# Prompt logits of a hybrid decoder step: keys as half and remainder on the two halves of the partitions, queries doubled

## What is computed

```python
def gqa_attend(q, k_sel, v_sel, valid):
    b, t = q.shape[0], q.shape[1]
    qg = q.reshape(b, t, N_KV_HEADS, GROUP, HEAD_DIM).astype(jnp.float32)
    s = jnp.einsum('btngd,btknd->btngk', qg, k_sel.astype(jnp.float32)) * (HEAD_DIM ** -0.5)
    s = jnp.where(valid[:, :, None, None, :], s, -jnp.inf)
    p = jax.nn.softmax(s, axis=-1)
    o = jnp.einsum('btngk,btknd->btngd', p, v_sel.astype(jnp.float32))
    return o.reshape(b, t, ATTN_DIM).astype(q.dtype)
```

## Time and profile before

| | us |
|---|---|
| median of 3 runs (2747.8 to 2750.54) | 2749.54 |
| span of the profiled execution | 2748.0 |
| TensorE busy | 2554.6 (93%) |
| VectorE busy | 1214.8 (44%) |
| ScalarE busy | 1112.5 (40%) |
| POOL busy | 1006.6 (37%) |

### The profile page before, as it was taken

One profiled execution on the slowest core, in us unless ns is written; L12 is line 12 of the kernel. 1 busy time (PEld: TensorE's weight loads), 2 busy tenths in 40 slices (PEclk: granted clock), 3 DMA queues, 4 the chain that ended last, 5 costly groups with the idle time before them and its releaser, 6 DMA issues.

```text
span 2748.0 us, 40635 instructions
## 1 busy us (share of the span) xinstructions
PE 2554.6 (93%) x15166; PEld 2233.7 (81%) x15166; DVE 1214.8 (44%) x3074; ACT 1112.5 (40%) x1833; POOL 1006.6 (37%) x527
## 2 busy tenths in 40 slices
PE   6999999999779988999989988898999999999997
PEld 6999998879657777867876887787889888878787
DVE  4232224628654344443545666565333234322344
ACT  4222223635424343345544544664443233322332
POOL 5333433324434444322542332221224354454340
PEclk9999999999889999999999999999999999999998
DMA  5323323332234454211322221111113222232222
GB/s 173 97 92 106 113 87 111 124 127 95 90 96 145 128 154 136 87 47 54 127 75 73 78 78 47 47 55 39 47 47 115 78 94 90 100 107 94 91 71 73
DMA packets 157030, 253.34 MB, mean 92 GB/s; under 512 B 15009, under 2 KB 101282, under 8 KB 156834
## 3 DMA queue, kind: packets, MB, share of 16 engines
q1 hardware_dynamic: 154144, 247.02, 27.7%
q10 hardware_dynamic: 2690, 3.72, 0.4%
HBM read 240.34 MB, written 18.73 MB: 94 GB/s over the span
## 4 chain that ended last, share of the span: by engine, by line
PE 73%; DVE 11%; ACT 7%; issue 4%; POOL 3%; DVEq 1%; DMA 1%; ACTq 0%; SPq 0%
PE ps L1594 22%; PE ps L1596 21%; PE ps L1595 21%; PE ps L1807 2%; PE ps L1863 2%; POOL w_lo L789 1%; PE ps L1793 1%; PE ps L1729 1%; DVE ps L1159 1%; ACT w_hi L890 1%; DVE ha_lo L1161 1%; POOL kv_kr L839 1%; ACT ha_hi L940 1%; DVE s_hits L1419 1%; DVE xa L1250 1%
## 5 line engine op out<-in xcount | busy, mean ns | idle before, releaser
L789 POOL TENSOR_TENSOR w_lo<-raw,w_hi 128x1024 fp32r<-128x1024 f32 x250 | 599.5, 2400 | 833.2 <-ACT w_hi L890 832.9
L1594 PE MATMUL ps<-xna_hi,w_hi 128*128 128x288 f32 x2000 | 606.6, 303 | 14.1 <-POOL xna_lo L795 7.3
L1595 PE MATMUL ps<-xna_lo,w_hi 128*128 128x288 f32 x2000 | 596.1, 298 | 0.0
L1596 PE MATMUL ps<-xna_hi,w_lo 128*128 128x288 f32 x2000 | 595.6, 298 | 0.0
L789 POOL TENSOR_TENSOR d_lo<-raw,d_hi 128x1024 fp32r<-128x1024 f32 x90 | 214.9, 2388 | 653.0 <-ACT d_hi L890 653.0
L1594 PE MATMUL ps<-xnb_hi,w_hi 128*128 128x512 f32 x1000 | 406.5, 406 | 0.0
L1594 PEld LDWEIGHTS ps<-xna_hi,w_hi 128*128 128x128 f32 x2000 | 382.6, 191 | 27.8 <-issue 17.6
L1596 PE MATMUL ps<-xnb_hi,w_lo 128*128 128x512 f32 x1000 | 394.5, 394 | 0.0
L1595 PE MATMUL ps<-xnb_lo,w_hi 128*128 128x512 f32 x1000 | 393.9, 394 | 0.0
L1595 PEld LDWEIGHTS ps<-xna_lo,w_hi 128*128 128x128 f32 x2000 | 382.4, 191 | 0.2
L1596 PEld LDWEIGHTS ps<-xna_hi,w_lo 128*128 128x128 f32 x2000 | 381.9, 191 | 0.0
(11 more groups left out here) (331 smaller groups left out, 4101.1 us busy)
## 6 DMA issues: line engine op xcount, KB each, us to landing
raw<-in_w_gu SPq DMA_DIRECT2D x176, 512.0 KB, 3.5
raw<-in_w_d SPq DMA_DIRECT2D x88, 512.0 KB, 3.5
raw<-in_w_ring SPq DMA_DIRECT2D x74, 512.0 KB, 3.5
pages<-in_vk_pages SPq DMA_DIRECT2D x256, 128.0 KB, 2.6
idx_flat<-in_idx_pages SPq DMA_DIRECT2D x256, 32.0 KB, 2.4
idxp<-idx_flat SPq DMA_DIRECT2D x8, 1024.0 KB, 6.7
x_spill<-xa SPq DMA_DIRECT2D x1, 2304.0 KB, 8.9
xa<-x_spill SPq DMA_DIRECT2D x4, 576.0 KB, 6.0
```

What stands on the lines that cost most here:

```text
L789: g_.tensor_tensor(lo[slot][:, :, :], raw[l % 2][:, :, :], hi[slot][:, :, :].bitcast(f32), ALU.subtract).then_inc(lo_done, 1)
L1594: mm(out, shi, mhi, start=first, stop=False)
L1595: mm(out, shi, mlo, start=False, stop=False)
L1596: return mm(out, slo, mhi, start=False, stop=last)
```

## The change

A key head now has a tensor of its own, `kT[h]`, with 128 partitions: the rounded half of the keys on the head's own 64 partitions, the remainder on the other 64. It takes the same space as `kT_hi` and `kT_lo`. The queries' rounded half lies twice, on both halves of the partitions, in `qb_hi`, arranged by head and tile; `qb_lo` has the remainder on the head's own half and zeros on the other. One matmul of 128 rows then gives hi x hi plus hi x lo, a second one lo x hi. `split_mm` is no longer used for the prompt's logits.

The queries are prepared by half blocks of two tiles, in two groups of events: "qb" (ScalarE, now four copies of 64 x 256 in each half) and "ql" (VectorE, two subtractions, and four zero fills ahead of blocks 0 and 4). They stand at steps 4 and 0, and the buffer is now one of a half instead of one of a block's parity, so that "qb" waits for the logits of the same half of the block before. The keys' copies are two for each chunk, and their remainders move from POOL to VectorE (`key_remainders`), ahead of the first rotation after the keys.

```diff
@@ -188,9 +188,11 @@
             pv = [("pv", *two)] if two else []
             if s == 0:
-                groups += [[("qb", now[0])], [], []]
+                groups += [[("qb", now[0], 0), ("qb", now[0], 1)], [("ql", now[0], 0), ("ql", now[0], 1)], []]
             elif now and now[1] == 4 and now[0] + 1 in blocks:
-                groups.append([("qb", now[0] + 1)])
+                groups += [[("qb", now[0] + 1, 0)], [("ql", now[0] + 1, 0)]]
+            elif now and now[1] == 0:
+                groups += [[("qb", now[0], 1)], [("ql", now[0], 1)]]
             for i in range(max(len(qk), len(tr), 1)):
...
@@ -288,7 +290,7 @@
         chosen = lambda name: [[("exact", name)], [("room", name)]] + [[(step, b)] for b in SEARCH[name] for step in ("ties", "pick")]
         side = [[("bt", "B1", j)] for j in range(EARLY, 32)] + chosen("B1")
-        side[-4].append(("qb", 4))
+        side[-4] += [("qb", 4, 0), ("qb", 4, 1)]
         late = [[("bt", "B2", j)] for j in range(32)] + chosen("B2")
...
@@ -506,7 +508,7 @@
         iwT = [at("iwT_a", [128, WIDTH[0]], f32, H + 4608), at("iwT_b", [128, WIDTH[1]], f32, H + 7680)]
         ikT = at("ikT", [128, SEQ], f32, P)
-        kT_hi, kT_lo = at("kT_hi", [128, SEQ], f32r, P + 4096), at("kT_lo", [128, SEQ], f32r, P + 8192)
+        kT = [at(f"kT{h}", [128, SEQ], f32r, P + 4096 + 4096 * h) for h in range(2)]
         V = at("V", [128, 8, 128], f32, P + 12288)
...
@@ -544,8 +546,8 @@
               [at(f"PT_b{s}", [128, 8, 128], f32, XNB + 8192 + 4096 * s) for s in range(2)]]
         q_at = (XNA + 8192, XNB + 16384)
-        qb_hi = [[at(f"qb_hi{g}{s}", [128, 4, 128], f32r, q_at[g] + 4096 * s) for s in range(2)] for g in range(2)]
-        qb_lo = [[at(f"qb_lo{g}{s}", [128, 4, 128], f32r, q_at[g] + 4096 * s + 2048) for s in range(2)] for g in range(2)]
+        qb_hi = [[at(f"qb_hi{g}{s}", [128, 2, 2, 128], f32r, q_at[g] + 4096 * s) for s in range(2)] for g in range(2)]
+        qb_lo = [[at(f"qb_lo{g}{s}", [128, 2, 2, 128], f32r, q_at[g] + 4096 * s + 2048) for s in range(2)] for g in range(2)]
         inv = [at("inv_a", [128, 128], f32, XNA + 16384), at("inv_b", [128, 128], f32, XNB + 24576)]
...
@@ -794,27 +796,10 @@
                     g_.tensor_tensor(xn_lo[g][:, m, own(c)], xnf[g][:, m, own(c)], xn_hi[g][:, m, own(c)].bitcast(f32), ALU.subtract).then_inc(xn_pool, 1)
 
-            def product(pn, half):
-                kind, w, c, key = products[pn]
-                if kind != "in" or half < PARTS[c] - 1 or key[0] != T_K:
-                    return
-                g, (o, k) = GROUP[c], CH[c]
-                first, at_ = FIRST[c], PPOS[c]
-                pool.wait_ge(k_hi_done, c + 1)
-                z = tb[2]
-                if c == 0:
-                    g_.tensor_tensor(kn_lo[:, :], z[:, 0:NS], kn_hi[:, :].bitcast(f32), ALU.subtract)
-                g_.tensor_tensor(kT_lo[:, at_:at_ + k - first], z[:, o + first:o + k], kT_hi[:, at_:at_ + k - first].bitcast(f32), ALU.subtract).then_inc(k_ready, 1)
-
             def pad(kc):
                 if kc == 0:
                     pool.wait_ge(xnf_done, n("scale", 1, 1, KT - 1))
                     g_.memset(S0[0:64, HALF:HW], NEG).then_inc(s0_pad, 1)
-
-            def queries(b):
-                g = group(b)
-                pool.wait_ge(q_hi_done, n("qb", b))
-                g_.tensor_tensor(qb_lo[g][b % 2][:, :, :], attn[g][:, :, lcol(b):lcol(b) + 128], qb_hi[g][b % 2][:, :, :].bitcast(f32), ALU.subtract).then_inc(q_ready, 1)
 
...
@@ -849,7 +834,7 @@
                 last.then_inc(pe_ready, 1)
 
-            does = {"begin": begin, "sp": split, "scale": scale, "p": product, "sil": pad, "qb": queries, "qs": sample_queries,
+            does = {"begin": begin, "sp": split, "scale": scale, "sil": pad, "qs": sample_queries,
                     "ks": keys, "mix": mix, "pe": embed}
...
@@ -967,7 +952,9 @@
                         if c == 0:
                             A(kn_hi[:, :], tb[2][:, 0:NS], ACT.Copy)
-                        A(kT_hi[:, at_:at_ + k - first], tb[2][:, o + first:o + k], ACT.Copy).then_inc(k_hi_done, 1)
+                        for h in range(2):
+                            last = A(kT[h][64 * h:64 * h + 64, at_:at_ + k - first], tb[2][64 * h:64 * h + 64, o + first:o + k], ACT.Copy)
+                        last.then_inc(k_hi_done, 1)
                 elif t == T_V:
...
@@ -1020,15 +1007,19 @@
                     A(vn[:, :], ps[0:NS, 7, 0:128], ACT.Copy).then_inc(v_copied, 1)
 
-            def queries(b):
+            def queries(b, half):
                 g = group(b)
                 if b == 0:
                     act.wait_ge(s_pv, total("vp"))
                 act.wait_ge(prod_done, last_in[g] + 1)
                 act.wait_ge(rope_done, n("rope", T_V - 1, CHUNKS[g][-1]))
-                if b - 2 in BLOCKS[g]:
-                    act.wait_ge(qk_done, n("qk", b - 2, 7, len(qk_pieces(b - 2)) - 1))
-                A(qb_hi[g][b % 2][:, :, :], attn[g][:, :, lcol(b):lcol(b) + 128], ACT.Copy).then_inc(q_hi_done, 1)
+                if b - 1 in BLOCKS[g]:
+                    act.wait_ge(qk_done, n("qk", b - 1, 4 * half + 3, len(qk_pieces(b - 1)) - 1))
+                for h in range(2):
+                    src = attn[g][64 * h:64 * h + 64, 2 * half:2 * half + 2, lcol(b):lcol(b) + 128]
+                    for to in range(2):
+                        last = A(qb_hi[g][half][64 * to:64 * to + 64, h, :, :], src, ACT.Copy)
+                last.then_inc(q_hi_done, 1)
 
...
@@ -1177,7 +1168,19 @@
                         convolve(pn, *conv_part(key[0]), c, g, z)
 
+            def key_remainders(c):
+                (o, k), first, at_, z = CH[c], FIRST[c], PPOS[c], tb[2]
+                dve.wait_ge(k_hi_done, c + 1)
+                if c == 0:
+                    v.tensor_tensor(kn_lo[:, :], z[:, 0:NS], kn_hi[:, :].bitcast(f32), ALU.subtract)
+                for h in range(2):
+                    own_, other, cols = slice(64 * h, 64 * h + 64), slice(64 - 64 * h, 128 - 64 * h), slice(at_, at_ + k - first)
+                    last = v.tensor_tensor(kT[h][other, cols], z[own_, o + first:o + k], kT[h][own_, cols].bitcast(f32), ALU.subtract)
+                last.then_inc(k_ready, 1)
+
             def rotate(pn, t, c, g, z):
+                if t == T_K + 1:
+                    key_remainders(c)
                 zt, zs = (tb[0], tb[1]) if t % 2 == 0 else (tb[2], tb[3])
...
@@ -1506,6 +1509,19 @@
                 v.tensor_scalar(nb[:, s:s + 1], top, -0.125, None, ALU.mult).then_inc(nb_done, 1)
 
+            def queries(b, half):
+                g = group(b)
+                dve.wait_ge(q_hi_done, n("qb", b, half))
+                if b in (0, 4) and half == 0:
+                    for s in range(2):
+                        for h in range(2):
+                            v.memset(qb_lo[g][s][64 - 64 * h:128 - 64 * h, h, :, :].bitcast(f32), 0.0)
+                for h in range(2):
+                    rows = slice(64 * h, 64 * h + 64)
+                    last = v.tensor_tensor(qb_lo[g][half][rows, h, :, :], attn[g][rows, 2 * half:2 * half + 2, lcol(b):lcol(b) + 128],
+                                           qb_hi[g][half][rows, h, :, :].bitcast(f32), ALU.subtract)
+                last.then_inc(q_ready, 1)
+
             def inverse(b, r, i):
...
@@ -1576,7 +1592,7 @@
                     v.tensor_tensor(xn_lo[g][:, j, :], attn[g][:, j, :], xn_hi[g][:, j, :].bitcast(f32), ALU.subtract).then_inc(mixa_ready, 1)
 
-            does = {"begin": begin, "sq": square, "sums": sums, "diag": diagonals, "scale": scale, "p": product, "d": add,
+            does = {"begin": begin, "ql": queries, "sq": square, "sums": sums, "diag": diagonals, "scale": scale, "p": product, "d": add,
                     "iw": head_weights, "prep": prepare, "wm": head_matrix, "isc": index_scores, "bt": threshold_bit,
...
@@ -1767,17 +1783,17 @@
 
             def logits(b, r, i):
-                g, (rows, tile) = group(b), q_rows(r)
+                g, half, tile, h = group(b), r // 4, r // 2 % 2, r % 2
                 o, k = qk_pieces(b)[i]
-                if r == 0 and i == 0:
-                    pe.wait_ge(q_ready, n("qb", b))
+                if r % 4 == 0 and i == 0:
+                    pe.wait_ge(q_ready, n("ql", b, half))
                     pe.wait_ge(k_ready, CHUNKS[g][-1] + 1)
                     pe.wait_ge(v_copied, g + 2)
                     if b == 0:
                         pe.wait_ge(s_evac, total("kq"))
                 wait(pe, smax_done, n("qk", b, r, i) - 1)
-                split_mm(ps[:, 5, 0:k], qb_hi[g][b % 2][rows, tile, :], qb_lo[g][b % 2][rows, tile, :],
-                         kT_hi[rows, o:o + k], kT_lo[rows, o:o + k], True, True).then_inc(qk_done, 1)
+                mm(ps[:, 5, 0:k], qb_hi[g][half][:, h, tile, :], kT[h][:, o:o + k], start=True, stop=False)
+                mm(ps[:, 5, 0:k], qb_lo[g][half][:, h, tile, :], kT[h][:, o:o + k], start=False, stop=True).then_inc(qk_done, 1)
```

## The result

The changed kernel takes 2760.69 us (median of five runs, 2757.58 to 2766.24); the kernel before, beside it, 2750.54 (2747.8 to 2752.6). The ratio is 1.0038 with a 95% interval of 1.0026 to 1.0051: some 10 us slower, where 18 us faster was predicted, and outside the predicted range. The profiled execution took 2757.58 us and spans 2755.8.

The account below looks back on a forecast made before the run. TensorE, with 73% of the chain, was taken as the bound in the first and last logit stretches. 31.4 - 2.5 - 0.8 - 2 - 1 - 4 - 3 = 18.1 us faster gave 2731 us, range 2711 to 2748.

Parts of the forecast that it names:

- What bounds the kernel: TensorE is the bound in 1880 to 2065 us; in 1660 to 1880 it is busy only 190.5 of 220.
- One matmul of three: Prompt logits: dropping the third matmul of each of 96 logits saves 17.0 us of TensorE.
- the change of shape: Around logits: gaps of about 0.09 to 0.10 us between 64-row and 128-row matmuls go, 21.4 us together.
- How much of it reaches the end: Of 38.4 us saved on TensorE, 24.4 in first and third stretches plus 7 of 14.0 in the second: 31.4.
- The groups packed anew: Both weaves: 9 more groups each over the same places take cover from samples (4 us) and the shorter search (3).
- Remainders on VectorE: Query subtractions moved from POOL: 13.4 us in all, mostly beside TensorE's work; 2.5 us at block 4, 0.8 around 1180.
- The place without cover: First queries of block 4, queued in VectorE's run of ties, choice and search bits: 2.5 us.
- 8 us or grows by 2 to 3: Sign of being right: the wait ahead of block 4's logits, part of it now for query remainders on VectorE.
- ScalarE and the keys: Eight query copies a block cost 2 us (0 to 8), key preparation 1 (0 to 2); the copies' new waits nothing.
- The surplus stays: Logit gaps come from starting a PSUM group, not rows, so only 17 us is removed: 2748; chance 0.14.
- nearly all arrives: Cover suffices and stalls shorten with the logits: 38.4 us less 3 of VectorE's run, 2714; chance 0.14.
- VectorE meets POOL: Query subtractions stand while POOL runs its own, 2 us each; with 18 meetings 2767; chance 0.10.

Follow-up runs that it names:

- ms_again: Kernel before with two 128-row logit matmuls and ScalarE copying the transposes ahead of the exponential, run a second time: 2718.69 us, ratio 0.9877.
- p1: Kernel before with only the change's additional groups, left empty: 2765.15 us, ratio 1.0047.
- m1: Kernel before with only the logits' matmuls changed to two of 128 rows, old copies, remainders and groups: 2738.19 us, ratio 0.9939.
- bs: Kernel before with only ScalarE's copy of the transposed weights moved ahead of the same group's exponential: 2745.29 us, ratio 0.9965.

## Why the prediction was wrong, point by point

*What bounds the kernel.* That TensorE is the bound in 1880 to 2065 us was read rightly from its 181.1 of 185. What wasn't asked is how far behind the next engine was. The 0.08 us in hand ahead of the values stand in the trace of before, and they are used up by the first logit that gets shorter.

The forecast, 18.1 us faster, and the 10 us slower that were measured are 28 apart. By the experiments three terms of the sum make that up: the matmuls brought 17 instead of 31.4, the preparation cost 18 instead of 6.3, and the groups 9 to 13 instead of 7.

*One matmul of three, and the change of shape.* Right in each start-to-start distance. With 0.33 on the way into values too, in the version with the copy ahead: 1986.70 to 1987.03.

*How much of it reaches the end.* This is the step that failed first. The first and third stretches were counted whole, 24.4 us, because TensorE was busy there, and half of the second, 7. Alone the matmuls brought 17 us, not 31; in the first and third stretch 15.0. With the copy ahead they brought 25, nearer to the step's number, which silently assumed such an order. So the copy behind the exponential accounts for 8 of the 14 us that are missing; the rest stays open. The wait that the step did expect, for row maxima in the middle stretch, grew from 16.5 to 20.5 there (ms_again, 1640 to 1860 us):

```profile
PE ps L1782 <- DVE small L1501: 20.5, 9, 8.2
```

*The groups packed anew.* 7 us were allowed, for cover lost in the samples' stretch and the searches. The groups cost 13 in the kernel before and 9 in the change, and not there: the wait for key remainders, which should have grown by a few us, fell from 26.9 to

```profile
PE ps L1610 <- POOL kv_kr L824: 23.2, 19, 4.2
```

What was left out is that more groups over the same places make two groups share one. Counted from the lists, 17 groups share a place in the first weave (8 before), and 7 in the second (none before). Such a pair in the last stretch:

```profile
2007.05 0.60 PE L1809 MATMUL ps<-ident,Sx_b 128*128 128x128 f32 x4
...
2008.00 0.50 PE L1795 MATMUL ps<-kT,qb_hi 128*128 128x512 f32 x1 [0.36 <-DVE small L1501]
...
2010.19 1.96 PE L1823 MATMUL ps<-PT_b,V 128*64 128x128 f32 x16 [1.46 <-ACT PT_b L1042]
```

No product lies between the steps, so TensorE meets the whole chain of maximum, exponential and copy: 0.36 and 1.46 us. That these pairs carry the cost is not shown: no version has as many groups without shared places, and in p1 the idle time over the span didn't grow; its longer busy time came with the lower granted clock.

*Remainders on VectorE.* The usual duration was right: 422 ns median, 0.42 predicted. The place without cover was named rightly. VectorE's work there was priced too low, 2.5 us; it took 1.36 and 3.59, 4.95 together. What it costs TensorE was priced about rightly: two waits, 4.37 and 6.42, stand where one of 7.66 was the earlier trace rows, 3.1 us more, and the sign "8 us or grows by 2 to 3, part of it now for query remainders" came:

```profile
1665.50 1.36 DVE L1518 MEMSET qb_lo<- 64x256 f32 x4
1666.79 3.59 DVE L1521 TENSOR_TENSOR qb_lo<-attn_b,qb_hi 64x256 fp32r<-64x256 f32 x4
...
1669.55 0.41 PE L1795 MATMUL ps<-kT,qb_hi 128*128 128x320 f32 x1 [4.37 <-DVE qb_lo L1521]
...
1676.53 0.63 PE L1795 MATMUL ps<-kT,qb_hi 128*128 128x320 f32 x1 [6.42 <-DVE small L1501]
```

The runs with the remainders alone put the whole at 8.5 us, where 3.3 were taken; the 5 us beyond are not at this place.

*ScalarE and the keys.* A copy took 0.41 to 0.42 us, as predicted. Their cost, with the fills, would be some 7 us by difference, near the upper bound of 8 rather than the 2 taken, but no run shows it. One term was put at nothing that wasn't: VectorE stands 11.1 us, five times, for these copies. The prediction let it pass because ScalarE is ahead in the first stretch; four of the five are there. At one of them, 1193.43, VectorE stood 3.17 us, and TensorE then waits 2.19 for the maximum behind it. The keys' 1 us isn't contradicted.

*The rivals.* None was it. "The surplus stays" and "nearly all arrives" fell at once, by the starts above and by m1. "VectorE meets POOL" names a number near the result, 2767, but not its cause: of the 32 subtractions four took over 1 us, each begun while POOL's weight remainder ran, and all together they lost about 5 us (mean 0.58 against 0.42). One of the four is in the run at block 4: 2.27 us, beginning inside this one of POOL:

```profile
1666.44 2.34 POOL L791 TENSOR_TENSOR d_lo<-raw,d_hi 128x1024 fp32r<-128x1024 f32 x1 [3.98 <-ACT d_hi L875]
```

This agrees with the Trainium skill, "SBUF — State Buffer", "SBUF: two separate sides": the later of the two engines stands until the other is done.

What the text had named as the sign of its failure, TensorE waiting in blocks 6 and 7, is just what came. The rival that was missing is the prediction's own price with another late engine: ScalarE's copy behind the exponential, which holds the values. And one sum is off: the forecast, the full gain and a tenth of the other two come to 0.78, not 0.82, for faster.

## What to carry to other kernels

A busy share near 98% doesn't say that time taken from an engine comes off: measure, at the step itself, by how much each operand was ready ahead of its use, and count a saving only up to that, plus what the late chain itself gains; here it was 0.08 us against 0.92, and 0.32 arrived. When an in-order engine serves two chains, serve first what the bounding engine needs next: one swap on ScalarE turned a loss of 10 us into a gain of 13. But give the old kernel the same swap before you credit the change: 10 of the 13 were there without it. A new wait is a cost only as far as it is longer than the one whose place it takes. Where a planner spreads groups over places, count how many come to share one: at the pair shown here the cover was gone altogether.

## What was not expected of the hardware

A wait can be followed by slower matmuls. In p1_packing_only the same 16 matmuls of attention values take 1.96 us at one step and 3.38 after a wait of 1.24:

```profile
2002.94 1.96 PE L1809 MATMUL ps<-PT_b,V 128*64 128x128 f32 x16
...
2011.16 3.38 PE L1809 MATMUL ps<-PT_b,V 128*64 128x128 f32 x16 [1.24 <-ACT PT_b L1053]
```

The granted clock was 1.00 in the first (2002.9 to 2004.7) and 0.55, thus mostly 1.2 GHz, in the second (2011.1 to 2014.4). In the changed kernel the wait of 1.46 us at 2010.19 left it at 1.00. Which waits bring it about stays open.

Over the span it matters. In three profiled executions the same 15166 matmuls kept TensorE busy 2554.6, 2560.8 and 2564.9 us (before, bs, p1) at mean granted clocks of 0.972, 0.968 and 0.967. And times of one kernel go with it: of 48 executions of the kernel before beside the experiments the nine at 0.972 took 2747.9 to 2751.7 us, the three at 0.966 to 0.968 2758.4 to 2759.6. The five of the changed kernel lay at 0.962 to 0.967; three of them, at 0.967, took 2757.6 to 2760.7, no more than the kernel before does there. So much of the 10 us by which the change is slower comes with a lower clock: an estimate, from the means of 0.970 and 0.966 and the 1.9 us that a thousandth of clock is worth over the 48 executions, is 8 us. It isn't the cause of all: with the copy ahead the change lies at the same mean of 0.966 and is 23 us faster.
